# The end of the state space part in two halves of eight heads, with the carried state ahead of the last diagonal product

## The chip, the cores and the metric
One core of one Trainium2 chip. The metric is the device time of one launch in microseconds; the lower the better.

## The reference
Two models run one after the other on 256 tokens of width 1024, all in float32: a first block of two layers (differential attention, latent attention and a state space branch side by side, then a gated feed-forward part), and a second block of one layer with two attention mixers and a mixture of experts. The change touches the end of the state space branch in each of the two layers of the first block. It has 16 heads of 64 values in 4 groups, a state of 128, and two chunks of 128 tokens:

```python
cs = jnp.cumsum(dt * a, axis=2)                                    # per chunk of 128 tokens
decay = jnp.exp(jnp.where(causal, cs[l] - cs[s], -inf))
y_diag = einsum('bclsgr,bcsgrp->bclgrp', cb[..., None] * decay, xdt)
states = einsum('bclgn,bclgrp->bcgrpn', bm, xdt * exp(cs[-1] - cs))
prev   = the state carried into the chunk (zero for chunk 0)
y_off  = einsum('bclgn,bcgrpn->bclgrp', cm, prev) * jnp.exp(cs)[..., None]
ys = y_diag + y_off + ssm_d * xs
ys = ys * silu(z)
ys = rmsnorm(ys in 4 groups of 256) * ssm_norm
...
merged = ga * (ya @ w_branch_a) + gb * (yb @ w_branch_b) + gc * (ys @ w_branch_c)
x = x + g_m * (merged @ w_out)
```

## The kernel before, in words
The five engines' programs are written out by hand; semaphores order them. Each engine runs its list strictly in order, so a wait holds up all that stands behind it on that engine.

**Weights** pass through a ring of four slots of 2 MB (`ring`), filled by SyncE in the order of `LAYER_CHUNKS`: ..., bb, gc0, gc1, bc0, bc1, ada10, wo0, ada11, wo1, up0, ... A slot is filled again when TensorE has finished the chunk four places earlier: wo0's load is issued when all four pieces of gc1 are done, ada10's when those of gc0 are.

**Gate pieces.** `gate_pieces(name, first, last)` makes pieces of 128 columns of a gate's projection (8 contraction steps of 128x256 each, which the trace shows as 16 records at L705). They depend on nothing of the state space part, and the program uses them as work for TensorE while VectorE and ScalarE prepare the next step. ScalarE's `gate(...)` turns them into tanh values (L1275). The pieces alternate between two PSUM buffers, `acc[0]` (gc0, bc0) and `acc[1]` (gc1, bc1).

**The state space part** goes through four quarters `hc` (chunk `t = hc // 2` of the tokens, eight heads each). For each quarter VectorE makes masked decay rows (`decay_rows`, L1913), TensorE spreads them (`decays`, L892, into `aux`), VectorE subtracts and clips (L1944, L1946), ScalarE takes the exponential (`seg_exps`, L1426), VectorE multiplies by C times B (L1959, `m_ready`), TensorE multiplies by x dt (`diagonal`, L904, into `aux2`), VectorE adds the result to `y` (L1968, `y_out`). After the second quarter TensorE makes the state of chunk 0 (L922), which ScalarE copies to SBUF (`stT`, L1224, `st_out`). `cb(1)` (L884) is the C times B product of chunk 1.

**The end.** After the last diagonal product TensorE multiplies C of chunk 1 by the carried state (L937, into both banks of `aux`, `yo_full`). VectorE scales chunk 0 by its root (`norm_y(0)`, L1929 and L1932), multiplies the product by its decay (L1975, 1024 elements, all 16 heads; result in the memory of `E`), adds it to `y` of chunk 1 (L1977), gates it (`gate_y(1)`, L1924). ScalarE squares it in four groups of 256 (`squares_y`, L1432) and takes the root (`root_y`, L1244); VectorE scales it (`norm_y(1)`). TensorE transposes chunk 0 as eight tiles and chunk 1 as eight tiles, in two signals of four (`transposes`, L628), all into `aux`. ScalarE takes all eight of chunk 0 and the last four of chunk 1 (`take_ysT`, L1444), VectorE the first four of chunk 1 (L1982). Then come the products with w_branch_c, bc0 and bc1 (L705), then wo0 and wo1, then the norm of the feed-forward part (`norm_root`: squares L1241, sum on TensorE L644, root L1244).

ScalarE holds one set of function tables at a time; a change of set shows as ACT_TABLE_LOAD at the line of the function that needs it. Tanh and exp are used side by side without one; a square root behind a tanh has one.

The functions that the change touches, and what calls them:

Of the kernel before, what the change touches and what calls it, by code (L numbers as in the profile page):

```python
# [9 lines left out]
ALU = mybir.AluOpType  # L10
ACT = mybir.ActivationFunctionType
# [213 lines left out]
def program(nc, a, consts, put_rows, out):  # L225

    ctx = ExitStack()
    with ctx:
# [3 lines left out]
        def sem(name):  # L232
            return ctx.enter_context(nc.semaphore(name))
# [220 lines left out]
        tria_ready, r_full, seg_ready, seg_exp, m_ready, y_full, y_out = (  # L454
            sem(n) for n in ("tria_ready", "r_full", "seg_ready", "seg_exp", "m_ready", "y_full", "y_out"))
        st_full, st_out, yo_full, yo_out = (sem(n) for n in ("st_full", "st_out", "yo_full", "yo_out"))
        y_gated, y_rt, y_n, ysT_t, ysT_out = (sem(n) for n in ("y_gated", "y_rt", "y_n", "ysT_t", "ysT_out"))
        merged_b, merged = sem("merged_b"), sem("merged")
        u_tap, u_silu, act_ready = (sem(n) for n in ("u_tap", "u_silu", "act_ready"))

# [163 lines left out]
        def _(pe):  # L624
# [61 lines left out]
            for l in range(DEPTH):  # L686
# [237 lines left out]
                mm.then_inc(st_full, 1)  # L924
                pe.wait_ge(y_out, 4 * l + 2)
                cb(1)
                gate_pieces("gc0", 2, 4)
                pe.wait_ge(st_out, l + 1)
                decays(2)
                gate_pieces("gc1", 0, 2)  # L930
                diagonal(2)
                decays(3)
                gate_pieces("gc1", 2, 4)
                diagonal(3)

                for g in range(SM_G):
                    mm = pe.matmul(aux[:, SEQ * g:SEQ * g + SEQ], xb[:, 12 + g, P:2 * P], stT[:, SEQ * g:SEQ * g + SEQ],  # L937
                                   start=True, stop=True)
                mm.then_inc(yo_full, 1)
                pe.wait_ge(y_n, 2 * l + 1)  # L940
                pe.wait_ge(yo_out, l + 1)
                transposes([(y[:, 0, P * k:P * k + P], aux[:, P * k:P * k + P]) for k in range(KT)], ysT_t)
                pe.wait_ge(y_n, 2 * l + 2)
                pe.wait_ge(ysT_out, 3 * l + 1)
                for k0 in (0, 4):
                    transposes([(y[:, 1, P * k:P * k + P], aux[:, P * k:P * k + P]) for k in range(k0, k0 + 4)], ysT_t)
                pe.wait_ge(ysT_out, 3 * l + 3)
                for i in range(2):
                    w = shaped(arrived(f"bc{i}"), KT, 512)
                    open_acc(f"bc{i}")  # L950
# [271 lines left out]
        def _(act_):  # L1222
# [30 lines left out]
            for l in range(DEPTH):  # L1253
# [174 lines left out]
                def squares_y(t):  # L1428

                    act.wait_ge(y_gated, 2 * l + t + 1)  # L1430
                    for g in range(SM_G):
# [4 lines left out]
                def root_y(t):  # L1436
                    root(rs[:, SM_G * t:SM_G * t + SM_G], ss[:, SM_G * t:SM_G * t + SM_G], D // SM_G, (y_rt, 1))

                def take_ysT(turn, k0, k1):

                    t = turn // 2
                    act.wait_ge(ysT_t, 3 * l + turn)
                    for k in range(k0, k1):
                        last = act.activation(ysT[:, k, P * t:P * t + P], aux[:, P * k:P * k + P], ACT.Copy, scale=cc[:, V_SN + k:V_SN + k + 1])  # L1444
                    last.then_inc(ysT_out, 1)

                seg_exps(0)
# [2 lines left out]
                gate("gc0", 0, 2)  # L1450
                act.wait_ge(st_full, l + 1)
                copy(stT, aux).then_inc(st_out, 1)
                gate("gc0", 2, 4)
                seg_exps(2)
                gate("gc1", 0, 2)
                squares_y(0)
                seg_exps(3)
                gate("gc1", 2, 4)
                root_y(0)
                take_ysT(1, 0, KT)  # L1460
                squares_y(1)
                root_y(1)
                take_ysT(3, 4, KT)


                norm_root()
# [134 lines left out]
        def _(dve):  # L1601
# [89 lines left out]
            for l in range(DEPTH):  # L1691
# [231 lines left out]
                def gate_y(t):  # L1923
                    stt(y[:, t, :], y[:, t, :], 0.5, zb[:, t, :], ALU.mult, ALU.mult).then_inc(y_gated, 1)  # L1924

                def norm_y(t):

                    dve.wait_ge(y_rt, 2 * l + t + 1)
                    dve.reciprocal(rs[:, SM_G * t:SM_G * t + SM_G], rs[:, SM_G * t:SM_G * t + SM_G])  # L1929
                    D_()  # L1930
                    groups = y[:, t, :].rearrange("p (g n) -> p g n", g=SM_G)
                    tt(groups, groups, bc(rs[:, SM_G * t:SM_G * t + SM_G], 2, D // SM_G), ALU.mult).then_inc(y_n, 1)  # L1932

                decay_rows(0)
                dve.wait_ge(xs_out, 2 * l + 2)
# [4 lines left out]
                for hc in range(4):  # L1940
                    t, h0 = hc // 2, 8 * (hc % 2)

                    dve.wait_ge(r_full, 4 * l + hc + 1)
                    tt(E, shaped(aux, 8, P), bc(csb[:, t, h0:h0 + 8], 2, P), ALU.subtract)  # L1944
                    D_()
                    ts(E, E, 0.0, None, ALU.min).then_inc(seg_ready, 1)  # L1946
                    if hc < 3:
                        decay_rows(hc + 1)
                    half_y, half_x = y[:, t, SM_D * h0:SM_D * (h0 + 8)], xs[:, t, SM_D * h0:SM_D * (h0 + 8)]
                    tt(shaped(half_y, 8, SM_D), shaped(half_x, 8, SM_D), bc(rc[:, R_SD + h0:R_SD + h0 + 8], 2, SM_D), ALU.mult)  # L1950
                    D_()
                    dve.wait_ge(seg_exp, 4 * l + hc + 1)
                    if t == 0:

                        tt(xe[:, h0:h0 + 8, :], shaped(xdt[:, t, SM_D * h0:SM_D * (h0 + 8)], 8, SM_D),
                           E[:, :, P - 1:P].to_broadcast([P, 8, SM_D]), ALU.mult)
                        D_()
                    groups = E.rearrange("p (g r) n -> p g r n", g=2)
                    tt(groups, groups, bc(cbm[:, h0 // 4:h0 // 4 + 2, :], 2, 4), ALU.mult).then_inc(m_ready, 1)  # L1959
                    if hc == 0:  # L1960
                        branch_b(1)
                        D_()
                        g0, g1 = (gates[:, n].rearrange("p k n -> p (k n)") for n in range(2))
                        tt(g0, g0, g1, ALU.add).then_inc(merged_b, 1)
                    if hc == 2:
                        gate_y(0)
                    dve.wait_ge(y_full, 4 * l + hc + 1)
                    tt(half_y, half_y, aux2, ALU.add).then_inc(y_out, 1)  # L1968
                    if hc == 1:
                        take_cb(1)  # L1970
                norm_y(0)
                dve.wait_ge(yo_full, l + 1)
                dve.wait_ge(ecs_out, l + 1)
                off = E.rearrange("p h n -> p (h n)")
                tt(shaped(off, SM_H, SM_D), shaped(aux, SM_H, SM_D), bc(ecs[:, 1, :], 2, SM_D), ALU.mult).then_inc(yo_out, 1)  # L1975
                D_()
                tt(y[:, 1, :], y[:, 1, :], off, ALU.add)  # L1977
                D_()
                gate_y(1)
                norm_y(1)  # L1980
                dve.wait_ge(ysT_t, 3 * l + 2)
                tt(ysT[:, 0:4, P:2 * P], shaped(aux[:, 0:512], 4, P), bc(cc[:, V_SN:V_SN + 4], 2, P), ALU.mult).then_inc(ysT_out, 1)  # L1982
                dve.wait_ge(ada_done, 12 * l + ADA_AHEAD + 6)
                tt(mod[:, 16:40], pmod[:, 16:40], cc[:, V_ADA + 16:V_ADA + 40], ALU.add)
                D_()
# [313 lines left out]
```

## Time and profile before

| | us |
|---|---|
| runs of the kernel before | 2065.04, 2065.59, 2069.67; median 2065.59 |
| the profiled execution | 2066.68 |
| its span, first to last instruction | 2064.9 |
| TensorE busy in it | 1934.5 (94%) |
| VectorE busy | 643.5 (31%) |
| ScalarE busy | 416.3 (20%) |
| mean granted clock of TensorE | 0.964 of 2.4 GHz |

A busy TensorE is not one at its peak: the same matmul takes longer at the lower granted clock. The state space part's end stands at 340 to 382 us of the span in layer 0 and at 994 to 1036 us in layer 1. The rows below are one timeline per engine (start, duration, engine, line, operation, what it writes and reads, count, and in brackets the idle time before it with what ended it), and windows with the granted clock.

### The profile page before, as it was taken

How to read it: one execution, taken by the hardware profiler on the slowest of the kernel's cores; microseconds unless marked ns; L12 is line 12 of the kernel's file. 1: busy time of each engine (PE TensorE's matmuls, PEld its weight loads, DVE VectorE, ACT ScalarE, POOL GpSimd, SP SyncE). 2: the span in 40 equal slices, each digit the busy share in tenths (PEclk: the TensorE clock that was granted, in tenths of full speed). 3: DMA queues.
4: the chain of work that ended last, by engine and by line, in shares of the span. 5: the costliest groups of instructions: out<-in, count | busy, mean ns of one | idle time of the engine just before them, and what ended most of it. 6: DMA issues, size and time to landing. Idle time of an engine off the chain costs nothing.

```text
span 2064.9 us, 20975 instructions
## 1 busy us (share of the span) xinstructions
PE 1934.5 (94%) x8952; PEld 1385.5 (67%) x8952; DVE 643.5 (31%) x1121; ACT 416.3 (20%) x875; POOL 0.8 (0%) x9
## 2 busy tenths in 40 slices
PE   6989999889999999999899999998789999999996
PEld 3467788778888557688787888855664444444443
DVE  4442276333232435138532321033241111111111
ACT  3253121112110233312202211014311101111111
POOL 0000000000000000000000000000000000000000
PEclk9999999999999999999989999999779999999998
DMA  9733364264447473336335543453229999999970
GB/s 385 243 130 123 123 220 147 82 203 156 137 156 260 168 237 108 123 123 245 122 123 163 163 144 143 144 186 123 82 82 389 427 428 428 426 428 428 426 325 21
DMA packets 147229, 442.20 MB, mean 214 GB/s; under 512 B 8768, under 2 KB 58176, under 8 KB 133440
## 3 DMA queue, kind: packets, MB, share of 16 engines
q1 hardware_dynamic: 144704, 437.08, 56.2%
q10 hardware_dynamic: 2432, 3.78, 0.5%
q8 instruction: 71, 1.16, 0.2%
q14 instruction: 22, 0.18, 0.0%
HBM read 439.00 MB, written 1.84 MB: 213 GB/s over the span
## 4 chain that ended last, share of the span: by engine, by line
PE 89%; ACT 4%; DVE 3%; issue 1%; DVEq 1%; DMA 1%; PEld 0%; PEldq 0%; ACTq 0%
PE acc L705 36%; PE acc L1125 11%; PE acc L715 8%; PE aux L1142 6%; PE acc L978 4%; PE aux L978 4%; PE acc L1111 3%; PE acc L1002 3%; PE aux L628 3%; PE acc L1150 2%; PE aux L1150 1%; PE acc L1080 1%; PE aux L644 1%; PE aux L1065 1%; PE aux L810 1%
## 5 line engine op out<-in xcount | busy, mean ns | idle before, releaser
L705 PE MATMUL acc<-hT,ring 128*128 128x256 f32 x2688 | 594.0, 383 | 7.1 <-ACT hT L1300 7.1
L705 PEld LDWEIGHTS acc<-hT,ring 128*128 128x128 f32 x2688 | 514.6, 192 | 82.5 <-issue 12.0
L1125 PE MATMUL acc<-ring,yT 128*64 128x512 f32 (+1 forms) x528 | 176.2, 594 | 0.0
L715 PE MATMUL acc<-ring,hT 128*128 128x512 f32 (+1 forms) x384 | 166.7, 592 | 5.8 <-ACT hT L1300 5.8
L2015 DVE SCALAR_TENSOR_TENSOR area<-acc,vectors,area 128x255 f32<-128x255 f32 (+1 forms) x176 | 72.7, 475 | 214.3 <-ACT area L1471 212.6
L715 PEld LDWEIGHTS acc<-ring,hT 128*128 128x128 f32 x384 | 73.2, 193 | 89.7 <-issue 88.1
L2240 DVE TENSOR_TENSOR xT<-xT,acc 128x1024 f32<-128x1024 f32 x17 | 20.8, 1221 | 325.4 <-PE aux L1150 325.4
L1125 PE MATMUL acc<-area,yT 128*64 128x512 f32 x384 | 112.9, 594 | 0.0
L628 PE MATMUL aux<-kc,area 128*128 128x128 f32 (+1 forms) x412 | 63.0, 300 | 46.6 <-DVE area L1932 11.5
L1125 PEld LDWEIGHTS acc<-ring,yT 128*64 128x64 f32 (+1 forms) x528 | 55.5, 138 | 75.3 <-issue 75.3
L1142 PE MATMUL aux<-ring,area 128*64 128x512 f32 (+1 forms) x272 | 92.1, 595 | 1.4 <-ACT area L1224 1.4
L1224 ACT ACTIVATE area<-aux 128x512 f32<-128x512 f32 (+3 forms) x67 | 43.6, 682 | 246.5 <-PE aux L628 240.9
L628 PEld LDWEIGHTS aux<-kc,area 128*128 128x128 f32 (+1 forms) x412 | 52.4, 154 | 57.7 <-DVE area L1932 11.9
L978 PE MATMUL acc<-area,ring 128*128 128x256 f32 x352 | 83.2, 379 | 0.0
L978 PE MATMUL aux<-area,ring 128*128 128x256 f32 x352 | 83.2, 379 | 0.0
L1471 ACT ACTIVATE area<-acc,vectors 128x256 f32<-128x256 f32 x88 | 44.9, 560 | 180.3 <-PE acc L705 180.3
L1111 PEld LDWEIGHTS acc<-hT,zb 128*128 128x128 f32 x544 | 66.2, 199 | 15.5 <-issue 15.5
L1665 DVE SCALAR_TENSOR_TENSOR zb<-ring,cact,zb 128x512 f32<-128x512 f32 x98 | 73.7, 752 | 8.5 <-issue 1.4
L1111 PE MATMUL acc<-hT,zb 128*128 128x128 f32 x544 | 70.5, 286 | 3.2 <-DVE hT L2192 3.2
L978 PEld LDWEIGHTS aux<-area,ring 128*128 128x128 f32 x352 | 66.9, 190 | 9.1
L978 PEld LDWEIGHTS acc<-area,ring 128*128 128x128 f32 x352 | 66.8, 190 | 9.0
L1241 ACT ACTIVATE area<-xT 128x1024 f32<-128x1024 f32 x10 | 10.5, 1055 | 274.0 <-DVEq L1724 273.9
(357 smaller groups left out, 2108.8 us busy)
## 6 DMA issues: line engine op xcount, KB each, us to landing
ring<-in_w_in SPq DMA_DIRECT2D x34, 2048.0 KB, 10.2
ring<-in_ada_w SPq DMA_DIRECT2D x24, 2048.0 KB, 8.0
ring<-in_ffn_w_up SPq DMA_DIRECT2D x44, 1024.0 KB, 7.7
ring<-in_w_up SPq DMA_DIRECT2D x17, 2048.0 KB, 19.1
ring<-in_w_down SPq DMA_DIRECT2D x17, 2048.0 KB, 18.6
ring<-in_w_gate SPq DMA_DIRECT2D x16, 2048.0 KB, 15.7
area<-in_w_up SPq DMA_DIRECT2D x12, 2048.0 KB, 19.4
area<-in_w_down SPq DMA_DIRECT2D x12, 2048.0 KB, 18.0
```

What stands on the lines that cost most here:

```text
L628: last = pe.transpose(dst, src, ident[0:n, 0:n])
L705: mm = pe.matmul(acc[LU.buf[use]][:, SEQ * j:SEQ * j + SEQ], w[:, k, c0:c0 + P], x[:, k, :], start=(k == 0), stop=(k == n - 1))
L715: mm = pe.matmul(acc[LU.buf[use]][:, at:at + width], x[:, k, P * t:P * t + P], w[:, k, :], start=(k == 0), stop=(k == n - 1))
L978: mm = pe.matmul(dst, w[:, k - k0, P * f:P * f + P], act[:, k, :], start=(k == 0 and f % 2 == 0), stop=(k == FT - 1), skip_group_check=True)
L1002: mm = pe.matmul(acc[b][:, 512 * t:512 * t + width], hT[:, k, P * t:P * t + P], w[:, k, :], start=(k == 0), stop=(k == KT - 1))
L1111: mm = pe.matmul(acc[bank][:, P * k:P * k + P], h2t[:, t, P * k:P * k + P], pm[:, b, t].rearrange("p e c -> p (e c)"), start=(t == 0), sto ...
L1125: mm = pe.matmul(dst[rows_ * e:rows_ * e + rows_, :], xg[:, b, k, rows_ * e:rows_ * e + rows_], w[:, k, :], start=(k == 0), stop=(k == KT ...
L1142: mm = pe.matmul(aux[rows_ * e:rows_ * e + rows_, 512 * n:512 * n + 512], heT[:, k, rows_ * e:rows_ * e + rows_], w[:, k, 512 * n:512 * n ...
L1150: mm = pe.matmul((acc[bank], aux)[k // 4][:, SEQ * (k % 4):SEQ * (k % 4) + SEQ], ygs[:, P * k:P * k + P], pmT[:, b, :], start=True, stop=True)
L1471: act.activation(u4[:, i % 2, j, :], full(f"up{i}", j | 1)[:, SEQ * j:SEQ * j + SEQ], ACT.Identity, scale=cc[:, V_FW + 4 * FT + f:V_FW + 4 ...
L1665: last = stt(part, w[:, k, :], cact[:, k:k + 1], part, ALU.mult, ALU.add)
L2015: last = stt(u4[:, i % 2, j, d:], acc[LU.buf[f"up{i}"]][:, SEQ * j:SEQ * j + SEQ - d], cc[:, V_FW + 2 * FT * k + f:V_FW + 2 * FT * k + f + ...
```

## The change
TensorE's list between `cb(1)` and the products with w_branch_c is reordered: the second pair of gc0 goes behind decays(2), the first pair of gc1 behind decays(3), the product with the carried state ahead of diagonal(3), the third piece of gc1 behind diagonal(3), and its fourth piece between the transposes of chunk 1. VectorE takes the carried state, the sum and the gate of chunk 1 in two halves of eight heads, the first of them ahead of the last diagonal result; `norm_y(0)` moves behind both. Squares, roots and scaling of chunk 1 are in two parts as well. The first four transposes of chunk 1 go to `aux2`; VectorE takes the last four of both chunks (`ysT_late`), ScalarE the first four of both. ScalarE's tanh of the last pair of gc1 moves behind all roots and copies.

```diff
 # TensorE
                 cb(1)
-                gate_pieces("gc0", 2, 4)
                 pe.wait_ge(st_out, l + 1)
                 decays(2)
-                gate_pieces("gc1", 0, 2)
+                gate_pieces("gc0", 2, 4)
                 diagonal(2)
                 decays(3)
-                gate_pieces("gc1", 2, 4)
-                diagonal(3)
+                gate_pieces("gc1", 0, 2)
+                pe.wait_ge(seg_ready, 4 * l + 4)
                 for g in range(SM_G):
                     mm = pe.matmul(aux[:, SEQ * g:SEQ * g + SEQ], xb[:, 12 + g, P:2 * P], stT[:, SEQ * g:SEQ * g + SEQ],
                                    start=True, stop=True)
                 mm.then_inc(yo_full, 1)
-                pe.wait_ge(y_n, 2 * l + 1)
-                pe.wait_ge(yo_out, l + 1)
+                diagonal(3)
+                gate_pieces("gc1", 2, 3)
+                pe.wait_ge(y_n, 3 * l + 1)
+                pe.wait_ge(yo_out, 2 * l + 2)
                 transposes([(y[:, 0, P * k:P * k + P], aux[:, P * k:P * k + P]) for k in range(KT)], ysT_t)
-                pe.wait_ge(y_n, 2 * l + 2)
-                pe.wait_ge(ysT_out, 3 * l + 1)
-                for k0 in (0, 4):
-                    transposes([(y[:, 1, P * k:P * k + P], aux[:, P * k:P * k + P]) for k in range(k0, k0 + 4)], ysT_t)
-                pe.wait_ge(ysT_out, 3 * l + 3)
+                pe.wait_ge(y_n, 3 * l + 2)
+                pe.wait_ge(y_out, 4 * l + 4)
+                transposes([(y[:, 1, P * k:P * k + P], aux2[:, P * k:P * k + P]) for k in range(4)], ysT_t)
+                gate_pieces("gc1", 3, 4)
+                pe.wait_ge(y_n, 3 * l + 3)
+                pe.wait_ge(ysT_out, 2 * l + 1)
+                transposes([(y[:, 1, P * k:P * k + P], aux[:, P * (k - 4):P * (k - 4) + P]) for k in range(4, 8)], ysT_t)
+                pe.wait_ge(ysT_out, 2 * l + 2)
+                pe.wait_ge(ysT_late, 2 * l + 2)
 # ScalarE
                 copy(stT, aux).then_inc(st_out, 1)
+                seg_exps(2)
                 gate("gc0", 2, 4)
-                seg_exps(2)
-                gate("gc1", 0, 2)
                 squares_y(0)
                 seg_exps(3)
-                gate("gc1", 2, 4)
+                gate("gc1", 0, 2)
                 root_y(0)
-                take_ysT(1, 0, KT)
                 squares_y(1)
                 root_y(1)
-                take_ysT(3, 4, KT)
+                squares_y(2)
+                root_y(2)
+                take_ysT(1)
+                take_ysT(2)
+                gate("gc1", 2, 4)
 # VectorE
+                def add_state(half):
+                    off, at = xe.rearrange("p h n -> p (h n)")[:, 512 * half:512 * half + 512], 512 * half
+                    tt(shaped(off, 8, SM_D), shaped(aux[:, at:at + 512], 8, SM_D), bc(ecs[:, 1, 8 * half:8 * half + 8], 2, SM_D),
+                       ALU.mult).then_inc(yo_out, 1)
+                    D_()
+                    tt(y[:, 1, at:at + 512], y[:, 1, at:at + 512], off, ALU.add)
+                    D_()
+                    gate_y(1 + half)
...
                     if hc == 2:
                         gate_y(0)
+                    if hc == 3:
+                        dve.wait_ge(yo_full, l + 1)
+                        dve.wait_ge(ecs_out, l + 1)
+                        add_state(0)
                     dve.wait_ge(y_full, 4 * l + hc + 1)
                     tt(half_y, half_y, aux2, ALU.add).then_inc(y_out, 1)
...
+                D_()
+                add_state(1)
                 norm_y(0)
-                dve.wait_ge(yo_full, l + 1)
-                dve.wait_ge(ecs_out, l + 1)
-                off = E.rearrange("p h n -> p (h n)")
-                tt(shaped(off, SM_H, SM_D), shaped(aux, SM_H, SM_D), bc(ecs[:, 1, :], 2, SM_D), ALU.mult).then_inc(yo_out, 1)
-                D_()
-                tt(y[:, 1, :], y[:, 1, :], off, ALU.add)
-                D_()
-                gate_y(1)
                 norm_y(1)
-                dve.wait_ge(ysT_t, 3 * l + 2)
-                tt(ysT[:, 0:4, P:2 * P], shaped(aux[:, 0:512], 4, P), bc(cc[:, V_SN:V_SN + 4], 2, P), ALU.mult).then_inc(ysT_out, 1)
+                norm_y(2)
+                def scale_ysT(t, k0, src):
+                    tt(ysT[:, k0:k0 + 4, P * t:P * t + P], shaped(src, 4, P), bc(cc[:, V_SN + k0:V_SN + k0 + 4], 2, P), ALU.mult).then_inc(ysT_late, 1)
+                dve.wait_ge(ysT_t, 3 * l + 1)
+                scale_ysT(0, 4, aux[:, 512:1024])
+                dve.wait_ge(ysT_t, 3 * l + 3)
+                scale_ysT(1, 4, aux[:, 0:512])
```

`squares_y`, `root_y`, `gate_y` and `norm_y` take a part instead of a chunk: part 0 is chunk 0 whole, parts 1 and 2 are the halves of chunk 1 (512 elements, two groups each).

## Rows read from the trace of the kernel before

**Rows 1.** The page, chain that ended last: shares of the span by engine
```profile
PE 89%; ACT 4%; DVE 3%; issue 1%; DVEq 1%; DMA 1%; PEld 0%; PEldq 0%; ACTq 0%
```

**Rows 2.** Timeline, layer 0, TensorE: start us, duration us, engine, line, operation
```profile
340.52 7.07 PE L705 MATMUL acc<-hT,ring 128*128 128x256 f32 x32
...
347.43 1.88 PE L892 MATMUL aux<-area,ones 128*128 128x512 f32 x4
...
349.15 7.07 PE L705 MATMUL acc<-hT,ring 128*128 128x256 f32 x32
...
366.46 1.90 PE L904 MATMUL aux<-area 128*128 128x64 f32 x16
...
368.19 1.95 PE L937 MATMUL aux<-area 128*128 128x256 f32 x8
...
371.75 1.06 PE L628 MATMUL aux<-kc,area 128*128 128x128 f32 x8 [1.61 <-DVE area L1975]
...
378.54 1.97 PE L628 MATMUL aux<-kc,area 128*128 128x128 f32 x8 [5.73 <-DVE area L1932]
```

**Rows 3.** The same timeline, VectorE
```profile
353.15 1.23 DVE L1959 TENSOR_TENSOR area<-area 128x1024 f32<-128x1024 f32 x1
...
368.39 0.69 DVE L1968 TENSOR_TENSOR area<-area,aux 128x512 f32<-128x512 f32 x1 [4.29 <-PE aux L904]
...
369.00 0.17 DVE L1929 RECIPROCAL rs<-rs 128x4 f32<-128x4 f32 x1
369.24 1.23 DVE L1932 TENSOR_TENSOR area<-area,rs 128x1024 f32<-128x1024 f32 x1
```

**Rows 4.** The same timeline, ScalarE and SyncE's queue, and three stretches of two norms
```profile
339.83 1.02 ACT L1224 ACTIVATE area<-aux 128x1024 f32<-128x1024 f32 x1 [2.79 <-PE aux L922]
...
366.66 0.37 SPq L557 DMA_DIRECT2D ring<-in_w_out  x1
...
372.85 2.18 ACT L1444 ACTIVATE ysT<-aux,vectors 128x128 f32<-128x128 f32 x8 [3.92 <-PE aux L628]
...
374.86 0.46 ACT L1432 ACTIVATE area<-area 128x256 f32<-128x256 f32 x1
...
376.67 0.30 ACT L1244 ACTIVATE rs<-ss,epsc 128x4 f32<-128x4 f32 x1
...
447.92 0.47 ACT L1244 ACTIVATE rstd<-aux,epsc 128x256 f32<-128x256 f32 x1 [2.08 <-PE aux L644]
...
686.98 1.06 ACT L1241 ACTIVATE area<-xT 128x1024 f32<-128x1024 f32 x1 [0.72 <-DVEq L1724]
688.06 1.28 ACT L1244 ACT_TABLE_LOAD   x1
```

**Rows 5.** Timeline, TensorE: bc0 and bc1, then wo0, in layers 0 and 1
```profile
381.74 29.85 PE L705 MATMUL acc<-ysT,ring 128*128 128x256 f32 x128 [1.23 <-ACT ysT L1444]
...
414.21 14.08 PE L705 MATMUL acc<-gates,ring 128*128 128x256 f32 x64 [1.84 <-DVE gates L1993]
...
1035.54 30.61 PE L705 MATMUL acc<-ysT,ring 128*128 128x256 f32 x128 [1.23 <-ACT ysT L1444]
...
1068.78 15.55 PE L705 MATMUL acc<-gates,ring 128*128 128x256 f32 x64 [1.84 <-DVE gates L1993]
```

**Rows 6.** Windows: bounds, length, busy of five engines, granted clock, DMA share, GB/s
```profile
366.46:371.75 5.29, 3.68 (x26) 3.15 (x24) 3.19 (x5) 2.24 (x4) 0.00 (x0) 1.00 0.72 257
371.75:378.54 6.79, 1.06 (x9) 0.83 (x9) 3.80 (x4) 4.05 (x17) 0.00 (x0) 0.78 0.29 108
...
381.74:385.00 3.26, 3.26 (x8) 2.63 (x9) 0.00 (x0) 0.00 (x0) 0.00 (x0) 0.50 0.00 0
...
1065.00:1080.00 15.00, 13.16 (x59) 11.40 (x58) 8.10 (x10) 0.00 (x0) 0.00 (x0) 0.89 0.85 280
```

**Rows 7.** The page: GB/s that the DMA queues moved, in 40 equal slices
```profile
GB/s 385 243 130 123 123 220 147 82 203 156 137 156 260 168 237 108 123 123 245 122 123 163 163 144 143 144 186 123 82 82 389 427 428 428 426 428 428 426 325 21
```

More of the change, by code:

```diff
@@ L456, in program @@
         st_full, st_out, yo_full, yo_out = (sem(n) for n in ("st_full", "st_out", "yo_full", "yo_out"))
-        y_gated, y_rt, y_n, ysT_t, ysT_out = (sem(n) for n in ("y_gated", "y_rt", "y_n", "ysT_t", "ysT_out"))
+        y_gated, y_rt, y_n, ysT_t, ysT_out, ysT_late = (sem(n) for n in ("y_gated", "y_rt", "y_n", "ysT_t", "ysT_out", "ysT_late"))
         merged_b, merged = sem("merged_b"), sem("merged")
@@ L1426, in seg_exps, with squares_y @@
                     act.activation(E, E, ACT.Exp).then_inc(seg_exp, 1)
-                def squares_y(t):
-                    act.wait_ge(y_gated, 2 * l + t + 1)
-                    for g in range(SM_G):
+                def squares_y(part):
+                    t = part and 1
+                    act.wait_ge(y_gated, 3 * l + part + 1)
+                    for g in ((0, 1, 2, 3), (0, 1), (2, 3))[part]:
                         act.activation((th, sqy)[t][:, 256 * g:256 * g + 256], y[:, t, 256 * g:256 * g + 256], ACT.Square,
@@ L1434, in squares_y, with root_y, take_ysT @@
                     act.drain()
[L1436 to L1441, printed above, removed]
+                def root_y(part):
+                    c0, c1 = ((0, 4), (4, 6), (6, 8))[part]
+                    root(rs[:, c0:c1], ss[:, c0:c1], D // SM_G, (y_rt, 1))
+                def take_ysT(turn):
                     act.wait_ge(ysT_t, 3 * l + turn)
-                    for k in range(k0, k1):
-                        last = act.activation(ysT[:, k, P * t:P * t + P], aux[:, P * k:P * k + P], ACT.Copy, scale=cc[:, V_SN + k:V_SN + k + 1])
+                    t = turn > 1
+                    for k in range(4):
+                        last = act.activation(ysT[:, k, P * t:P * t + P], (aux, aux2)[t][:, P * k:P * k + P], ACT.Copy, scale=cc[:, V_SN + k:V_SN + k + 1])
                     last.then_inc(ysT_out, 1)
@@ L1921, in branch_b, with gate_y, norm_y @@
                     stt(part, part, 1.0, full(f"bb{u}", 3), ALU.add, ALU.mult).then_inc(*free(f"bb{u}"))
[L1923 to L1929, printed above, removed]
-                    D_()
-                    groups = y[:, t, :].rearrange("p (g n) -> p g n", g=SM_G)
-                    tt(groups, groups, bc(rs[:, SM_G * t:SM_G * t + SM_G], 2, D // SM_G), ALU.mult).then_inc(y_n, 1)
+                def gate_y(part):
+                    t, c0, c1 = ((0, 0, D), (1, 0, 512), (1, 512, D))[part]
+                    stt(y[:, t, c0:c1], y[:, t, c0:c1], 0.5, zb[:, t, c0:c1], ALU.mult, ALU.mult).then_inc(y_gated, 1)
+                def norm_y(part):
+                    t, g0, g1 = ((0, 0, 4), (1, 0, 2), (1, 2, 4))[part]
+                    dve.wait_ge(y_rt, 3 * l + part + 1)
+                    r_ = rs[:, SM_G * t + g0:SM_G * t + g1]
+                    dve.reciprocal(r_, r_)
+                    D_()
+                    groups = y[:, t, 256 * g0:256 * g1].rearrange("p (g n) -> p g n", g=g1 - g0)
+                    tt(groups, groups, bc(r_, 2, D // SM_G), ALU.mult).then_inc(y_n, 1)
+                def add_state(half):
[6 more added lines that the diff above has]
+                    gate_y(1 + half)
                 decay_rows(0)
```

## The prediction

> **What bounds the kernel now.** I read the chain that ended last, then the timeline of the last stretch of the state space part (TensorE, then VectorE and ScalarE), then the granted clock over the same stretch, first in layer 0 and then in layer 1, which runs the same program. The reader is to see in the chain that it runs over TensorE for 89% of the span [rows 1]: a microsecond in which TensorE stands still or runs at its lower clock is a microsecond of the kernel. In the timeline of TensorE one piece of a gate is half of 6.91 us (340.52 to 347.43, two pieces), so 3.46 us; a decay product 1.72 us (347.43 to 349.15); a diagonal product 1.73 us (366.46 to 368.19); the state product by its 8 records of 1.95 us, about 1.73 us to the next start as well [rows 2]. Behind the last state product, which ends at about 369.92, TensorE waits 1.6 us before the eight transposes at 371.75, 5.73 us before the eight at 378.54, and 1.2 us before the products with w_branch_c at 381.74 [rows 2, 5]. What it waits for is one serial walk over 128 tokens by 16 heads: add the diagonal result, multiply the carried state by its decay, add, gate, square, root, scale, each pass some 1.2 us on VectorE or 1.8 us on ScalarE [rows 3, 4].
> The windows show the second half of the price. The granted clock of TensorE is 1.00 (2.4 GHz) up to the long wait, 0.78 on average in 371.75 to 378.54, and 0.50 (1.2 GHz) in the first 3.26 us of the w_branch_c products [rows 6]. Full clock would give the 128 records of bc0 and bc1 four times 6.91 us plus a tail of 0.16, 27.8 us; they took 29.85 us in layer 0 and 30.61 us in layer 1 [rows 5]. The excess is 2.05 and 2.81 us.
>
> **The change part by part, in layer 0's times.** I carry the profile's start times forward through the new order.
> (a) The second pair of gc0 no longer stands between cb(1) and decays(2). decays(2) must wait for ScalarE's copy of the state, which starts at 339.83 and takes 1.02 us, so it starts at about 340.92 where the gate pieces started at 340.52: 0.40 us lost, formerly hidden by these pieces [rows 2, 4].
> (b) gc0's pair then covers the decay chain of quarter 2. That chain runs from 347.43 to 353.15 + 1.23, 6.95 us after the decay product's start [rows 2, 3]; after the change it ends at 347.87, and decays (1.72) plus the pair (6.91) bring TensorE to the diagonal at 349.55. No stall, 1.7 us of room. With decays(3) at 351.28 and the first pair of gc1 at 353.00, quarter 3 is ready at about 357.6 (its chain is shorter: no decay rows are made in it) and TensorE is free at 359.91. The bound from the other side: if the longer chain held here too, it would be 358.2, still covered. Cost zero.
> (c) The state product starts at 359.91, the diagonal at 361.64, one gate piece at 363.37, which ends at 366.83. VectorE, idle by then, gets the carried state at about 361.85 (0.20 us after its last matmul's slot, as 368.19 to 368.39 shows [rows 2, 3]). Half a pass of 512 elements costs 0.69 us, by the addition of 512 at 368.39 [rows 3]; a drain between dependent passes 0.07 (369.00 + 0.17 to 369.24), and independent passes overlap by 0.08 (368.39 + 0.69 against 369.00) [rows 3]. add_state(0): 361.85 to 362.54, 362.61 to 363.30, gate 363.37 to 364.06. The diagonal's result, there at 363.57, is added until 364.67. add_state(1): 364.74 to 365.43, to 366.19, to 366.95. All three passes of the first half are done before the diagonal's addition could matter, which is what the two halves buy.
> (d) norm_y(0) stands behind both halves: reciprocal 0.17, drain, 1.23 of scaling [rows 3], so y of chunk 0 is ready at about 368.35. TensorE has been free since 366.83: 1.6 us idle (368.40). This wait is the new largest one. Before the change norm_y(0) was done at 370.47 and hidden by its neighbours; here it is not hidden. Its square and root are early: squares of chunk 0 follow gate_y(0), and the root's table load falls behind the first pair of gc1 at 360.6.
> (e) ScalarE squares a half in about 0.9 us (1.81 for four groups, 374.86 to 376.67) and roots it in 0.30 [rows 4]: first half 364.1 to 365.4, second 367.0 to 368.3. VectorE reaches norm_y(1) at 368.3 and norm_y(2) at 369.2, later than both roots. VectorE is therefore the only limit: norm_y(1) ends at 369.2 to 369.3, norm_y(2) at 370.1.
> (f) Eight transposes of chunk 0 issue in 0.85 us (1.06 with their tail [rows 2]): 368.40 to 369.25; the four of chunk 1 follow at 369.30 and gc1's last piece at 369.73, to 373.19. It covers norm_y(2) and both copies on ScalarE (1.1 us each, half of 2.18 [rows 4]). The last four transposes take 0.43 us, their result lands at 373.9, one pass of 0.69 us on VectorE, and bc0 starts at 374.6. In this tail TensorE idles 1.0 us.
> Against 381.74 that is 7.1 us earlier. Check by idle time: before 1.6 + 5.73 + 1.2 = 8.5 us, and 0.9 us by transposes at half clock; after 0.4 + 1.6 + 1.0 = 3.0, whose difference is 6.4; the rest is the slots between the last records and the next start (transposes 1.97 to 0.86), within 0.7. I take 7.1 and keep 6.4 as the low end of this term.
> (g) The lower clock after the long wait goes away if no wait of over 1.6 us is left: 2.05 us in layer 0 and 2.81 in layer 1 [rows 5].
> (h) Against it: a short wait can also bring the clock down. Ahead of wo0 TensorE has a few one-column matmuls and 1.84 us of idle in both layers; in layer 0 the 64 records behind took 14.08 us, in layer 1 15.55 at a window clock of 0.89 [rows 5, 6]. So 1.47 us, in one of two. The new gap, 1.6 us and then 1.3 us of short transposes, is of this kind. I charge 1.5 us once, bounds zero and twice 2.81.
> (i) Tables of ScalarE. The last pair of gc1 (tanh) now stands behind the roots, so two more table loads fall in each layer, one before this tanh, one before the root of the next norm. A load takes 1.28 us and starts directly behind the squares (686.98 + 1.06 to 688.06), ahead of the root's wait for TensorE's sum [rows 4]. The next norm's root waits 2.08 us for TensorE at 447.92 [rows 4], so 0.8 us of room remain: cost zero. Were that cover gone, it would be 1.28 us a layer. The first of the two loads has 13.8 us before bc1 opens the buffer of gc1.
> The Trainium skill speaks against this edit: ScalarE: Activation LUTs, "What ACT_TABLE_LOAD costs", puts a switch of table set at about 2.66 us, 1283 ns of load and the rest a drain. The trace agrees on the load (1.28 us) and shows no such drain before it (0.02 us between the squares and the load). By the page's figure 0.6 us would show in each layer, an estimate from it, and the sum would be 1.2 us worse.
> (j) Loads. wo0's weights are issued when gc1 is finished, at 366.66 before [rows 4], now at about 373.2; they are wanted after bc0 and bc1, about 30 us later, and in the slices of this part the queue moves 82 to 203 GB/s of the 428 that it reaches later [rows 7], so 2 MB land within some 10 us. Hidden; it would decide only from 30 us on.
>
> **The sum.** Two layers at 7.1 is 14.2 us, the clock gives 2.05 + 2.81 = 4.9 us, one short fall takes 1.5: 17.6 us. The profiled execution took 2066.68 us (span 2064.9 and 1.8 around it), 1.1 above the median of the runs. 2066.7 - 17.6 = 2049.1, and carried to the median of 2065.59, 2048.0. I forecast 2048.
>
> **Rivals.** (A) The clock falls in both layers in spite of the shorter wait, as it did behind 1.84 us in layer 1 [rows 5, 6], and costs what it cost before: the gain is the 14.2 us of starts, or 2051.4, down to 12.8 (2052.8) with the low end of 6.4. Against it: in 366.46 to 371.75, which holds the wait of 1.6 us, the granted clock stayed 1.00 [rows 6].
> (B) The VectorE chain between the last diagonal and norm_y(0) is longer than the passes add up to: it holds nine passes, each dependent on a drain. If a half pass costs nearly a whole one (0.69 to 1.22), TensorE waits some 3.2 us longer in each layer (six half passes, 0.53 each), and the clock falls in both, some 2.4 us each and not 1.5 once: 17.6 - 6.4 - 3.3 is 7.9, 2057.7. For it: VectorE is the only limit there; against it: 0.69 us at 368.39 is a measured half pass out of PSUM.
> (C) The gain is given back further on: the loads of the experts run at over 425 GB/s in seven of the last slices [rows 7], and were they timed from the program's start, no microsecond before them would count: 2065.6. Against it stand the two slices of 82 GB/s ahead of them, in which the loads wait for the compute, so their start moves with it.
> (D) Slower than before: the gaps bring TensorE to 1.2 GHz and the gate pieces that used to separate the waits are spent, so that it stays low through bc0 and bc1. Each of the 27.6 us of these two would then cost as much again. In the trace the products behind the longest wait ran low for twice their excess, 4.1 and 5.6 us [rows 5]. This rival decides from 18 us of low clock in each layer (9 us lost against 9 gained), and its full price is 27.6 - 7.1 - 2.4, 18 us a layer: 2102.
>
> **How the numbers follow.** The forecast's own case (gain 15.5 to 20) has 0.58, A 0.18, B 0.11, C 0.06, D 0.02, and 0.05 for a gain of over 20 (no fall at all, and the later norms at a better clock). 0.2% is 4.1 us, about what a measurement of this kernel can tell from no change. Faster by more holds in the forecast, A, B and the last: 0.92. C gives the same: 0.06. D slower: 0.02. The low end of the range is the full 19.1 of the sum and 2.5 more (a pass that overlaps better, the fall in layer 1 ahead of wo0 gone too, 1.47 [rows 5]): 2044. The high end takes in A with its low term and part of B: 2054.
>
> **What would show it.** In the new profile TensorE waits 0.4 us before decays(2), about 1.6 us for L1932's successor (norm_y) before the first transposes, 1.0 us before bc0, and nothing over 2 us between. The products with w_branch_c start 7.1 us earlier and take 27.8 us instead of 29.85 and 30.61. If their 128 records still take 29.8 in both layers, A was right; if the wait before the first transposes is over 3 us, B; if the table load stands between squares and root of the next norm and TensorE's norm wait grows, (i) was wrong. The forecast fails if bc0 starts less than 5 us earlier, or if the time between bc0 and the end of the span changes by more than 5 us.

## The result, and the profile after
The changed kernel takes 2048.25 us in the median (2045.34 to 2053.33, 4 runs) against 2065.76 before (2065.04 to 2069.67): a ratio of 0.9914, 95% interval [0.9891, 0.9937]. Forecast were 2048.0 and the range 2044 to 2054. A second set of five runs gave 2045.60, ratio 0.9904 [0.9889, 0.9919]. Each ratio here and below is taken to the kernel before in the same set of rounds, over all its runs, so it is not the quotient of two medians. The profiled execution took 2048.62 us, its span is 2046.8, 18.1 us shorter than before.

TensorE in layer 0 from the C times B product of chunk 1 on, in the timeline of the changed kernel (start us, duration us, engine, line, operation, count, idle before it); it answers to [rows 2] and [rows 5]:

```profile
338.32 1.05 PE L884 MATMUL aux<-area 128*128 128x128 f32 x8
...
339.60 1.98 PE L892 MATMUL aux<-area,ones 128*128 128x512 f32 x4 [0.22 <-ACT area L1229]
...
358.74 1.89 PE L936 MATMUL aux<-area 128*128 128x256 f32 x8
...
360.46 1.89 PE L904 MATMUL aux<-area 128*128 128x64 f32 x16
...
362.19 3.67 PE L705 MATMUL acc<-hT,ring 128*128 128x256 f32 x16
...
367.28 1.53 PE L628 MATMUL aux<-kc,area 128*128 128x128 f32 x12 [1.42 <-DVE area L1944]
...
368.65 3.62 PE L705 MATMUL acc<-hT,ring 128*128 128x256 f32 x16
...
372.10 0.60 PE L628 MATMUL aux<-kc,area 128*128 128x128 f32 x4
...
373.53 27.86 PE L705 MATMUL acc<-ysT,ring 128*128 128x256 f32 x128 [0.83 <-issue]
401.24 0.95 PE L652 MATMUL pmod<-ones,zb 128*128 128x1 f32 x8
404.03 15.77 PE L705 MATMUL acc<-gates,ring 128*128 128x256 f32 x64 [1.84 <-DVE gates L2020]
```

The whole part stands 1.3 us earlier in this execution for reasons ahead of it, so I measure from the C times B product of chunk 1 (L884), which the table below calls the C times B product. To the start of bc0 it is 373.53 - 338.32 = 35.21 us, against 381.74 - 339.63 = 42.11 before, where that product is

```profile
339.63 1.05 PE L884 MATMUL aux<-area 128*128 128x128 f32 x8
```

The wait of 5.73 us is gone; 1.42 and 0.83 us are left, and 0.22 us ahead of decays(2). bc0 and bc1 take 27.86 us with their tail instead of 29.85. The windows show why (bounds, length, busy of five engines, granted clock, DMA share, GB/s); they answer to [rows 6]:

```profile
362.00:370.00 8.00, 6.58 (x39) 5.67 (x38) 6.96 (x13) 4.00 (x17) 0.00 (x0) 1.00 0.00 0
370.00:376.00 6.00, 5.17 (x27) 4.37 (x26) 0.95 (x3) 2.53 (x6) 0.00 (x0) 1.00 0.42 136
```

The granted clock stays at 1.00 (2.4 GHz) through both short waits. VectorE behind the state product, same columns as [rows 3]:

```profile
360.66 0.69 DVE L1949 TENSOR_TENSOR area<-aux,ecs 128x512 f32<-128x512 f32 x1 [4.29 <-PE aux L936]
...
361.45 0.69 DVE L1952 TENSOR_TENSOR area<-area 128x512 f32<-128x512 f32 x1
...
362.21 0.69 DVE L1934 SCALAR_TENSOR_TENSOR area<-area,zb 128x512 f32<-128x512 f32 x1
362.82 0.68 DVE L1994 TENSOR_TENSOR area<-area,aux 128x512 f32<-128x512 f32 x1
...
365.76 0.17 DVE L1941 RECIPROCAL rs<-rs 128x4 f32<-128x4 f32 x1
...
366.00 1.23 DVE L1944 TENSOR_TENSOR area<-area,rs 128x1024 f32<-128x1024 f32 x1
```

Each half pass costs 0.69 us, as counted, and what TensorE waits for at 367.28 is the scaling of chunk 0 (L1944), for which VectorE would have had time during its 4.29 us of idle ahead of L1949. It would need the root of chunk 0 earlier too: ScalarE has it only at 361.20, behind the tanh of gc1's first pair.

```profile
360.90 0.30 ACT L1249 ACTIVATE rs<-ss,epsc 128x4 f32<-128x4 f32 x1
```

The next norm on ScalarE: its second squares before, and then the changed kernel, answering to 447.92 in [rows 4]:

```profile
444.78 1.06 ACT L1241 ACTIVATE area<-xT 128x1024 f32<-128x1024 f32 x1 [13.65 <-DVEq L1724]
...
436.28 1.06 ACT L1246 ACTIVATE area<-xT 128x1024 f32<-128x1024 f32 x1 [13.65 <-DVEq L1733]
437.35 1.28 ACT L1249 ACT_TABLE_LOAD   x1
439.42 0.47 ACT L1249 ACTIVATE rstd<-aux,epsc 128x256 f32<-128x256 f32 x1 [0.78 <-PE aux L644]
```

The new table load starts 0.01 us behind the squares, and the root still waits 0.78 us for TensorE: hidden. From the second squares to the root it is 3.14 us, before and after.

**Where the 18.1 us are.** Starts of bc0: 6.90 us in each layer, 13.8. bc0 with bc1, start to start of the next: 29.68 to 27.71 and 30.45 to 27.70, together 4.7. wo0: 13.92 to 15.60 in layer 0 and 15.39 to 13.92 in layer 1, together -0.2. The rest is outside the changed lines: 1.3 and 2.8 us less ahead of the two places, 4.3 more behind them (from the end of layer 1's wo0 to the end of the span 985.0 us against 980.7). Of the 4.3, 3.0 arise in one stretch of the second block, where the same 128 records took longer at a lower granted clock. The changed kernel first, then before, each with the window from 250 to 300 us behind the end of layer 1's wo0:

```profile
1311.80:1361.80 50.00, 44.10 (x126) 25.81 (x125) 17.16 (x32) 8.18 (x16) 0.00 (x0) 0.90 0.55 205
1327.61 51.34 PE L1007 MATMUL acc<-ring,hT 128*128 128x512 f32 x128 [3.01 <-DVE hT L2064]
...
1334.17:1384.17 50.00, 44.11 (x132) 25.89 (x131) 20.01 (x43) 8.18 (x16) 0.00 (x0) 0.97 0.54 201
1349.54 48.34 PE L1002 MATMUL acc<-ring,hT 128*128 128x512 f32 x128 [3.01 <-DVE hT L2037]
```

These 985.0 us stand in both profiles of the changed kernel. Eight profiles of seven other kernels, before's among them, have 980.6 to 980.9 us there, and three profiles of two others 987.1 to 987.2. The 128 records take 51.2 to 51.3 us in the five profiles with 985.0 or more and 48.3 us in the eight others, behind the same 3.01 us of idle. Why the clock falls there in some is open.

### The profile page after: what moved, and what is told of

The parts are those of the page before. It is cut to its first block, busy times and chain, and to the rows that moved or that the text cites. A ratio compares the mean times of both kernels' runs of the same rounds, so it can differ in the third digit from the quotient of the medians.

```text
span 2046.8 us, 20999 instructions
## 1 busy us (share of the span) xinstructions
PE 1929.9 (94%) x8952; PEld 1381.0 (67%) x8952; DVE 646.3 (32%) x1133; ACT 420.5 (21%) x873; POOL 0.8 (0%) x9
## 3 DMA queue, kind: packets, MB, share of 16 engines
HBM read 439.00 MB, written 1.84 MB: 215 GB/s over the span
## 4 chain that ended last, share of the span: by engine, by line
PE 90%; ACT 4%; DVE 4%; issue 1%; DVEq 1%; DMA 1%; PEld 0%; PEldq 0%; ACTq 0%
PE acc L705 36%; PE acc L1130 12%; PE acc L715 9%; PE aux L1147 6%; PE acc L983 4%; PE aux L983 4%; PE acc L1116 3%; PE acc L1007 3%; PE aux L628 3%; PE acc L1155 2%; PE aux L1155 1%; PE acc L1085 1%; PE aux L644 1%; PE aux L1070 1%; ACT area L1229 1%
## 5 line engine op out<-in xcount | busy, mean ns | idle before, releaser
L715 PE MATMUL acc<-ring,hT 128*128 128x512 f32 (+1 forms) x384 | 166.7, 592 | 5.8 <-ACT hT L1305 5.8
L1007 PE MATMUL acc<-ring,hT 128*128 128x512 f32 (+1 forms) x160 | 65.2, 570 | 3.0 <-DVE hT L2064 3.0
## 6 DMA issues: line engine op xcount, KB each, us to landing
ring<-in_w_in SPq DMA_DIRECT2D x34, 2048.0 KB, 10.2
ring<-in_ada_w SPq DMA_DIRECT2D x24, 2048.0 KB, 8.2
ring<-in_w_up SPq DMA_DIRECT2D x17, 2048.0 KB, 18.9
ring<-in_w_down SPq DMA_DIRECT2D x17, 2048.0 KB, 18.5
ring<-in_w_gate SPq DMA_DIRECT2D x16, 2048.0 KB, 15.5
area<-in_w_up SPq DMA_DIRECT2D x12, 2048.0 KB, 19.2
area<-in_w_down SPq DMA_DIRECT2D x12, 2048.0 KB, 17.9
```

The source lines that it names most:

```text
L715: mm = pe.matmul(acc[LU.buf[use]][:, at:at + width], x[:, k, P * t:P * t + P], w[:, k, :], start=(k == 0), stop=(k == n - 1))
L1007: mm = pe.matmul(acc[b][:, 512 * t:512 * t + width], hT[:, k, P * t:P * t + P], w[:, k, :], start=(k == 0), stop=(k == KT - 1))
```

## Experiments
One table for all: us from the C times B product to bc0, and bc0 with bc1 (start to start), from each kernel's profile, layer 0 / layer 1; then the medians.

| kernel | to bc0 | bc0 + bc1 | median us (runs) | ratio to before, 95% |
|---|---|---|---|---|
| before | 42.11 / 42.11 | 29.68 / 30.45 | 2065.76 (4) | |
| changed | 35.21 / 35.21 | 27.71 / 27.70 | 2048.25 (4) | 0.9914 [0.9891, 0.9937] |
| gates_only | 35.77 / 35.78 | 27.73 / 27.73 | 2047.69 (5) | 0.9914 [0.9901, 0.9927] |
| halves_only | 40.59 / 40.58 | 27.70 / 29.51 | 2064.37 (12) | 0.9998 [0.9986, 1.0011] |
| fill | 41.24 / 41.24 | 27.73 / 27.73 | 2058.35 (5) | 0.9966 [0.9953, 0.9979] |
| state_behind | 36.40 / 38.07 | 27.70 / 27.70 | 2052.88 (5) | 0.9934 [0.9921, 0.9947] |
| norm_early | 33.79 / 33.79 | 27.70 / 27.70 | 2047.84 (6) | 0.9922 [0.9908, 0.9936] |
| late_wait | 34.22 / 34.21 | 27.62 / 27.63 | 2046.10 (5) | 0.9904 [0.9890, 0.9918] |
| norm_late | 32.80 / 32.80 | 27.63 / 27.62 | 2042.44 (4) | 0.9893 [0.9878, 0.9907] |
| after_again | 35.21 / 35.21 | 27.70 / 27.70 | 2045.60 (5) | 0.9904 [0.9889, 0.9919] |
| norm_late_again | 32.80 / 32.80 | 27.63 / 27.63 | 2041.74 (4) | 0.9885 [0.9870, 0.9900] |
| gates_norm_late | 34.69 / 34.69 | 27.73 / 27.73 | 2045.58 (4) | 0.9900 [0.9885, 0.9915] |

The distance to bc0 repeats to 0.01 us between two executions of one kernel; the median of the changed kernel moved by 2.7 us between two sets, for reasons elsewhere (see halves_look). So the starts decide what an edit does to this part. The column of bc0 with bc1 need not repeat once the clock has fallen: see halves_only and halves_look.

**gates_only**, the order of the gate pieces alone (TensorE's list is shown; ScalarE's tanh of the three moved pairs moves with them, the last pair behind all roots and copies):

```diff
                 cb(1)
-                gate_pieces("gc0", 2, 4)
                 pe.wait_ge(st_out, l + 1)
                 decays(2)
-                gate_pieces("gc1", 0, 2)
+                gate_pieces("gc0", 2, 4)
                 diagonal(2)
                 decays(3)
-                gate_pieces("gc1", 2, 4)
+                gate_pieces("gc1", 0, 2)
                 diagonal(3)
...
                 transposes([... chunk 0 ...], ysT_t)
+                gate_pieces("gc1", 2, 4)
                 pe.wait_ge(y_n, 2 * l + 2)
```

> The kernel before with the gate pieces alone moved: gc0's second pair behind decays(2), gc1's first pair behind decays(3), gc1's second pair between the transposes of chunk 0 and of chunk 1; ScalarE's tanh of that pair last. No halves, state product behind the last diagonal product. Theory 'cover' (the gain is the gate pieces put into the long wait, and with it TensorE's full clock): the diagonal starts 6.5 us earlier, the wait of 1.6 us before the first transposes stays, the one of 5.7 is filled, bc0 starts 6.4 us earlier than before in each layer and takes 27.8 us; 2048 to 2050. Rival 'halves' (the gain needs the chain of chunk 1 cut in two and started ahead of the last diagonal product): at most a third of the gain, 2059 or more, with a wait of over 3 us left before the second transposes.

bc0 starts 6.34 us earlier (counted: 6.4) and the clock holds:

```profile
367.00 1.06 PE L628 MATMUL aux<-kc,area 128*128 128x128 f32 x8 [1.61 <-DVE area L1975]
367.90 7.07 PE L705 MATMUL acc<-hT,ring 128*128 128x256 f32 x32
374.81 1.04 PE L628 MATMUL aux<-kc,area 128*128 128x128 f32 x8
377.08 27.89 PE L705 MATMUL acc<-ysT,ring 128*128 128x256 f32 x128 [1.23 <-ACT ysT L1444]
```

The pair stands in the wait and fills it; no idle time is left before the second transposes. By the starts 6.34 of the 6.90 us are here. The ratio is the whole one, but that equality is in part chance: the changed kernel's profile lost 4.3 us behind the second place that gates_only's did not (985.0 against 980.9 us). "Cover" holds, "halves" falls.

**halves_only**, the changed kernel with the gate pieces where they were (gc0's second pair behind cb(1), gc1's pairs behind decays(2) and decays(3)), all else as changed.

> The changed kernel with the gate pieces back in their old places: halves, state product ahead of the last diagonal product, transposes in three parts, but no gate piece behind the diagonal. Theory 'cover': TensorE waits about 5 us before the transposes of chunk 0 and some 1.5 us more before bc0, bc0 starts some 3.1 us earlier than before, the granted clock falls again and bc0 with bc1 take 29.5 to 30.7 us; 2058 to 2061. Rival 'halves': most of the gain is here, below 2053.

```profile
373.03 2.82 PE L628 MATMUL aux<-kc,area 128*128 128x128 f32 x12 [4.92 <-DVE area L1943]
376.32 1.09 PE L628 MATMUL aux<-kc,area 128*128 128x128 f32 x4 [0.47 <-ACT ysT L1450]
378.24 27.86 PE L705 MATMUL acc<-ysT,ring 128*128 128x256 f32 x128 [0.83 <-issue]
```

The wait of 4.92 us is as expected, but bc0 starts 1.52 us earlier and not 3.1: I had counted the transposes at the full clock, and twelve of them took 2.82 us where the changed kernel needs 1.53. The second half of the expectation failed in layer 0: there bc0 with bc1 took 27.70 us and not 29.5 to 30.7. The low stretch had passed before they began, in layer 1 it had not. Granted clock at the start of bc0, layer 0 and layer 1:

```profile
378.24:382.00 3.76, 3.76 (x18) 3.32 (x19) 0.17 (x1) 0.00 (x0) 0.00 (x0) 1.00 0.02 4
...
1025.64:1030.00 4.36, 4.36 (x12) 3.56 (x13) 0.17 (x1) 0.00 (x0) 0.00 (x0) 0.58 0.01 4
```

So this wait lowered the clock in both layers (the twelve transposes took 2.82 us in each), but what that costs depends on which matmuls the low stretch meets. The twelve runs fall into two groups, six at 2060.5 to 2060.9 and six at 2067.9 to 2069.5, so the median of 2064.4 says little. The lower group lies in the expected range by luck: the starts gave 3.2 us less than counted, layer 0's clock 1.8 to 3.0 us more. "Halves" falls here too, since neither group is below 2053.

**halves_look**, the same kernel once more.

> One more execution of halves_only, whose twelve were six at 2060.5 to 2060.9 and six at 2067.9 to 2069.5. If this one is of the upper group, its profile tells where the 8 us lie. Theory: TensorE's clock, which falls in one more or one fewer of its short waits; then the starts around the state space part agree with the first profile and the longer stretches have a granted clock below 1.00. Rival: a later start of bc0 in both layers.

It took 2069.69 us. Its starts around the part agree with the first profile (40.59 and 40.58 us). Of the 8.8 us of span, 4.5 lie before the C times B product of layer 0 (342.12 against 337.65), 2.7 between the layers (565.06 against 562.41 from wo0's end) and 1.7 in bc0 and bc1 of layer 0 (29.40 us against 27.70 behind the same wait of 4.92 us). Windows of the first profile, then of this one:

```profile
0.00:120.00 120.00, 97.66 (x374) 51.05 (x375) 51.44 (x100) 40.52 (x73) 0.78 (x9) 0.96 0.80 293
120.00:330.00 210.00, 204.53 (x994) 167.19 (x993) 100.43 (x166) 60.76 (x154) 0.00 (x0) 1.00 0.46 158
```

```profile
0.00:120.00 120.00, 97.56 (x358) 50.47 (x360) 51.37 (x100) 38.79 (x72) 0.78 (x9) 0.93 0.79 291
120.00:330.00 210.00, 204.53 (x997) 167.63 (x996) 96.03 (x163) 62.33 (x154) 0.00 (x0) 0.98 0.44 151
```

The granted clock is 0.93 and 0.98 where it was 0.96 and 1.00: the same program has more time at the lower clock. That fits the theory; which of its waits bring it, I did not follow.

**fill**, the kernel before with work for nobody in the long wait:

```diff
                 transposes([... chunk 0 ...], ysT_t)
+                for i in range(12):
+                    pe.matmul(pmod[:, 128:128 + SEQ], hT[:, i % KT, 0:P], hT[:, i % KT, :], start=True, stop=True)
                 pe.wait_ge(y_n, 2 * l + 2)
```

> The kernel before with 12 matmuls of 128x256 on hT, whose result nobody reads, between the transposes of chunk 0 and the wait for chunk 1: about 5.2 us of work inside the wait of 5.7 us, nothing else moved. If the lower clock behind the wait is a price of its own, the transposes at 378.5 take 1.06 us and bc0 with bc1 27.8 us, which saves 0.9 + 2.05 in layer 0 and 0.9 + 2.81 in layer 1, bc0 itself starting 0.9 us earlier: 2059 (2058 to 2061). If the clock has nothing to do with the wait, 2065 to 2066 and 29.8 us for bc0 with bc1.

```profile
369.78 1.06 PE L628 MATMUL aux<-kc,area 128*128 128x128 f32 x8 [1.61 <-DVE area L1977]
370.69 5.35 PE L944 MATMUL pmod<-hT 128*128 128x256 f32 x24
376.58 1.09 PE L628 MATMUL aux<-kc,area 128*128 128x128 f32 x8 [0.55 <-DVE area L1934]
378.91 27.89 PE L705 MATMUL acc<-ysT,ring 128*128 128x256 f32 x128 [1.23 <-ACT ysT L1446]
```

bc0 starts 0.87 us earlier, bc0 with bc1 fall to 27.73 us in both layers: by the starts 2 x 0.87 + 1.95 + 2.72 = 6.4 us, by the ratio 7, as expected. The low clock behind the wait is a price of its own, a third of the gain, and work with no use takes it away.

**state_behind**, the changed kernel with `diagonal(3)` ahead of the product with the carried state, and `add_state(0)` behind the addition of the diagonal result.

> The changed kernel with the product of the carried state behind the last diagonal product again, so that both halves of the carried state are added after it; all else as changed. My count: VectorE starts the first half 1.7 us later and adds the diagonal result first, so norm_y(0) ends 0.95 us later, TensorE waits 2.4 instead of 1.4 us before the first transposes, bc0 starts 0.9 to 1.0 us later in each layer: 1.9 us over the changed kernel's 2048.3. Rival: the order of the two products is worth nothing, because VectorE was idle before them: 0.

The wait grows from 1.42 to 2.61 us and bc0 starts 1.19 us later in layer 0. In layer 1 it starts 2.86 later, since there the clock fell:

```profile
1016.59 2.48 PE L628 MATMUL aux<-kc,area 128*128 128x128 f32 x12 [2.60 <-DVE area L1943]
1018.87 4.38 PE L705 MATMUL acc<-hT,ring 128*128 128x256 f32 x16
1023.09 0.60 PE L628 MATMUL aux<-kc,area 128*128 128x128 f32 x4
```

Sixteen records take 4.38 us where the changed kernel has 3.62. The order of the two products, with VectorE's first half behind it, is worth 1.2 us a layer where the clock holds. The fall that I had charged to a wait of 1.6 us appears at one of two waits of 2.6. I had expected 1.9 us in all and got 4.05 by the starts; the median is 4.6 us above the changed kernel's, which is of another set.

**norm_early, late_wait, norm_late.** norm_early moves the scaling of chunk 0 into VectorE's idle time:

```diff
 # ScalarE
                 seg_exps(3)
-                gate("gc1", 0, 2)
                 root_y(0)
...
-                gate("gc1", 2, 4)
+                gate("gc1", 0, 4)
 # VectorE
                     if hc == 3:
+                        norm_y(0)
                         dve.wait_ge(yo_full, l + 1)
...
                 add_state(1)
-                norm_y(0)
```

> The changed kernel with the scaling of chunk 0 (norm_y(0)) ahead of the wait for the carried state, where VectorE stands idle for 4.3 us, and for this the root of chunk 0 directly behind the last exponential on ScalarE and both tanh pairs of gc1 at the end of its list. Theory 'VectorE's chain is the limit behind the last diagonal product': the wait of 1.42 us before the first transposes goes, 0.2 us remains before the first four of chunk 1, bc0 starts 1.3 to 1.5 us earlier, 2.6 to 3 us in all: 2045.5. Rival 'the wait is for the second half of the carried state' : both products share aux, and the wait stays above 1 us.

late_wait moves the wait for `ysT_late` from before bc0 to before the fifth contraction step (k == 4) of its first piece.

> The changed kernel with one wait later: the first piece of bc0 waits for VectorE's copy of the last four transposes (ysT_late) ahead of its fifth contraction step only. Its first four steps read the tiles that ScalarE copied long before. The wait of 0.83 us before bc0 goes, bc0 starts 1.0 us after the last transposes' start less 0.4, 1.0 us earlier, and VectorE's copy lies beside its first 1.7 us: 2.0 us in all, 2046.3. Rival: the copy isn't done when the fifth step comes, and the wait only moves: 0.

> Both edits of norm_early and late_wait: they take away different waits, so the gains add, 4.6 to 5 us under the changed kernel: 2043.5. Rival: with two waits gone, the first one's end (VectorE's scaling of the second half) becomes late for the last transposes and takes a microsecond per layer back: 2045.5.

bc0 starts 1.42, 0.99 and 2.41 us earlier than in the changed kernel, in both layers: all three counts hold. In norm_late the timeline of TensorE marks no wait in the part but the 0.22 us for the state copy:

```profile
340.96 1.05 PE L884 MATMUL aux<-area 128*128 128x128 f32 x8
...
368.34 1.69 PE L628 MATMUL aux<-kc,area 128*128 128x128 f32 x12
...
373.76 3.62 PE L960 MATMUL acc<-ysT,ring 128*128 128x256 f32 x16
```

norm_early's median does not show its 2.8 us. Its profile has 2.2 us more than the changed kernel's behind the second place (987.2 against 985.0).

**after_again, norm_late_again, gates_norm_late**, side by side.

> The changed kernel itself, on the chip and in the rounds of the next two, so that these are compared with it and not with another day's runs: 2048 (2045 to 2053).

> norm_late beside the changed kernel. In the profiles bc0 starts 2.41 us earlier in each layer, 4.8 us in all: 2043 to 2044 against 2048. Rival: the difference between its 2042.4 and 2048.3 was another chip's and another hour's; then under 2 us.

> gates_only (no halves, state product behind the diagonal) with the same two edits as norm_late: the root and scaling of chunk 0 ahead of the last diagonal result, both tanh pairs of gc1 last, and bc0's first piece waiting for ScalarE's copy of the last four tiles at its fifth step. The transposes of chunk 0 start 1.3 us earlier, bc0 starts after VectorE's copy, 0.9 us earlier than after ScalarE's: from the C times B product to bc0 33.6 us, against 35.77 in gates_only, 35.21 in the changed kernel and 32.80 in norm_late; 2045. If the halves are what makes a short end possible, it stays at 35 us or more: 2048.

norm_late is 3.9 us under the changed kernel in the same rounds, 4.8 by its starts; its four runs (2040.83 to 2043.03) all lie below the changed kernel's five (2044.28 to 2050.07), so the rival of another chip falls. gates_norm_late takes 34.69 us and not the 33.6 that I expected: I let VectorE multiply the carried state directly after the diagonal result, but with the products in the old order it waits for it:

```profile
360.78 0.69 DVE L1976 TENSOR_TENSOR area<-area,aux 128x512 f32<-128x512 f32 x1 [2.43 <-PE aux L904]
362.56 1.22 DVE L1983 TENSOR_TENSOR area<-aux,ecs 128x1024 f32<-128x1024 f32 x1 [1.09 <-PE aux L936]
```

Here is what state ahead and halves are for, taken together with the transposes in three parts and the new division of the copies, which no run separates from them: alone they bring 1.5 us of start, beside the moved gate pieces 0.56 us; once the scaling of chunk 0 is out of the way, they are 1.9 us of start (34.69 against 32.80).

## Why the prediction was right
(a) to (f), the new order. Counted from the C times B product, the first transposes were to start after 28.8 us and did after 28.96; bc0 after 35.0, measured 35.21. The term was 7.1 us a layer and measures 6.90. decays(2) starts 0.39 us later than the gate pieces did, 0.40 expected. This part was reasoned from rows and came out as reasoned.
(d) held as named: the largest wait left is for norm_y(0), 1.42 us for 1.6. I costed it and did not see that its place is a choice; norm_early shows 1.42 us a layer in it.
(c) was right in size and wrong in weight. "Which is what the two halves buy" reads as if the gain hung on them; gates_only has 6.34 of 6.90 us without them.
(g) 4.86 us expected, 4.7 measured, and fill shows that it is the idle time, not the order, that makes it: with the old order and the wait filled, both layers take 27.73 us. A long wait does not always make it, though: behind 4.92 us in halves_only, layer 0 took 27.70.
(h) failed as an argument and cost little. No fall came at the new wait: in the changed kernel (two profiles), gates_only, late_wait and gates_norm_late, ten places with a wait of 1.4 to 1.6 us, bc0 and bc1 took 27.6 to 27.7 us each time. My model for it, the gap ahead of wo0, is another thing: it has one-column matmuls ahead of 1.84 us of idle, and in 26 cases over 13 profiles it slowed wo0 ten times, now in one layer, now in the other. The changed kernel's own 15.60 us there offset before's 15.39. Without the 1.5 us the sum would have been 19.1; the starts and bc0 with bc1 gave 18.5. The rest of the program took 0.4 back, which leaves 18.1 of span: 1.3 and 2.8 us gained ahead of the two places, 4.3 lost behind, 0.2 lost in wo0. None of these was in the sum.
**Where it was luck.** That the median came within 0.3 us of 2048.0 is luck. The 1.5 us charged for a fall that did not come were mostly made up by 0.6 us too much in (f) and (g) and 0.4 us lost elsewhere, and the second set of the same kernel has 2045.60. What the prediction earned is the range and the mechanism.
(i) held: the loads are hidden, with 0.78 us of room for 0.8 expected. By the Trainium skill's figure (ScalarE: Activation LUTs, "What ACT_TABLE_LOAD costs"), 2.66 us with a drain, an estimate of 0.6 us would have shown at the root. The trace has no such drain on either side of the load (at the root of chunk 0 the load ends at 360.88 and the root starts at 360.90), and the stretch from squares to root kept its 3.14 us. The measurement decides for 1.28 us here.
(j) held: no wait for the weights of wo0 appears, 1.84 us for VectorE's sum stands before it as it did. The load was issued at 372.30, for 373.2 expected, and wo0 starts at 404.03.
Of the rivals, A and D did not occur (27.7 us for bc0 with bc1 in both layers), B is excluded by the 0.69 us of each half pass, C by the 17 us that reached the end. B also said that each of nine passes depends on a drain; the rows show independent ones that overlap, as the reciprocal at 365.76 does.

## What to carry to other kernels
Before shortening a serial chain, look for work of the waiting engine that could stand inside the wait instead of ahead of an earlier one that is already covered: moving three pairs of independent pieces to later places gave 6.34 of the 6.90 us a layer by the starts. Then ask of each remaining wait whether an idle engine could have done earlier what it waits for, and whether all of the work behind it needs it; that gave the next 4.8 us by the starts, 3.9 by the medians. To judge edits of one or two microseconds, compare starts from a fixed point of the same profile, not medians of the whole; and look at the clock behind the edit as well, since the starts alone do not show it.

## What had not been expected of the hardware
Useless matmuls pay: 5.35 us of them inside a wait of 5.73 us made the kernel 6.4 us faster by its starts, because the transposes and the 128 records behind ran at 2.4 GHz. The price of a wait is not fixed: behind 4.92 us in halves_only and halves_look the transposes were slow in all four places, bc0 with bc1 in three. And two profiles of one program differ by 8.8 us of span, with a lower granted clock where they part (0.93 against 0.96 in the first 120 us), while the distance between two points with the same clock between them repeats to 0.01 us.
